# Seven block products for eight in the output product of two of four chunks, and low parts of input weights kept in memory

## What is computed

```python
h = _layer_norm(x) * (1 + scale[:, None]) + shift[:, None]
proj = h @ w_in
xa, ga, u, v, gb = jnp.split(proj, SPLITS, axis=-1)      # five times 512 columns
ya = _pool_mixer(xa, w_pool, pool_scale) * jax.nn.silu(ga)
yb = _sgu_mixer(jax.nn.gelu(u, approximate=False), jax.nn.gelu(v, approximate=False),
                sgu_ln_g, sgu_ln_b, w_sgu, b_sgu) * jax.nn.silu(gb)
y = jnp.concatenate([ya, yb], axis=-1) @ w_out
z = DEEPNORM_ALPHA * x + gate[:, None] * y
return _layer_norm(z) * ln_g + ln_b
```

## Time and profile before

| | us |
|---|---|
| median of 3 runs (673.91 to 674.61) | 673.99 |
| the profiled execution | 673.68 |
| its span in the profile | 671.6 |
| PE busy in the span | 659.8 (98%) |
| DVE busy | 516.1 (77%) |
| ACT busy | 235.1 (35%) |
| POOL busy | 61.7 (9%) |

### The profile page before, as it was taken

How to read it: one execution, slowest core, us unless ns; L and a number is a source line. 1 busy time by engine, 2 the same in 40 slices (tenths; PEclk the granted TensorE clock), 3 DMA queues, 4 the chain that set the end, 5 groups by cost and what they waited for, 6 DMA issues and landing times.

```text
span 671.6 us, 8845 instructions
## 1 busy us (share of the span) xinstructions
PE 659.8 (98%) x3103; PEld 551.3 (82%) x3103; DVE 516.1 (77%) x956; ACT 235.1 (35%) x307; POOL 61.7 (9%) x77
## 2 busy tenths in 40 slices
PE   8999999999999999999999999999999999999995
PEld 8888888877888888888888888888888888888884
DVE  5678898749969967766979968775977986656776
ACT  4424644316522333224722332322821333323300
POOL 2000110100002201100002201000002210000010
PEclk9999999999999999999999999999999999999999
DMA  8995643785334472288243562378343454224111
GB/s 340 365 332 233 219 153 116 163 228 189 125 111 141 126 258 86 95 116 322 96 156 100 180 248 65 106 94 332 102 148 90 162 205 159 104 79 154 52 63 62
DMA packets 34546, 108.73 MB, mean 162 GB/s; under 512 B 6573, under 2 KB 7633, under 8 KB 34514
## 3 DMA queue, kind: packets, MB, share of 16 engines
q1 hardware_dynamic: 34514, 108.31, 49.5%
HBM read 97.80 MB, written 10.50 MB: 161 GB/s over the span
## 4 chain that ended last, share of the span: by engine, by line
PE 95%; issue 2%; DVE 2%; ACT 0%; DMA 0%; POOLq 0%; POOL 0%; DVEq 0%
PE bank_b L1053 63%; PE bank_a L1053 25%; PE bank_a L1180 2%; PE bank_a L1140 1%; PE bank_b L1113 1%; PE bank_a L1171 1%; DVE w_low L656 1%; PE bank_b L1077 0%; DVE v_gelu L708 0%; PE bank_b L1171 0%; PE bank_b L1132 0%; PE bank_b L1104 0%; DMA vector_rows<-in_vectors 0%; ACT h_high L528 0%; ACT w_high L509 0%
## 5 line engine op out<-in xcount | busy, mean ns | idle before, releaser
L1053 PE MATMUL bank_b<-h_high,w_high 128*128 128x512 f32 x512 | 202.2, 395 | 0.2 <-DVE h_low L668 0.2
L1053 PE MATMUL bank_b<-h_low,w_high 128*128 128x512 f32 x512 | 199.3, 389 | 0.0
L1053 PE MATMUL bank_b<-h_high,w_low 128*128 128x512 f32 x512 | 199.3, 389 | 0.0
L661 DVE TENSOR_TENSOR w_low<-w_float,w_high 128x1024 fp32r<-128x1024 f32 x98 | 119.5, 1220 | 40.3 <-ACT w_high L518 40.2
L518 ACT ACTIVATE w_high<-w_float 128x1024 fp32r<-128x1024 f32 x98 | 103.4, 1056 | 130.5 <-DMA w_float<-in_w_units 57.2
L1053 PEld LDWEIGHTS bank_b<-h_high,w_high 128*128 128x128 f32 x512 | 96.2, 188 | 20.2 <-issue 1.1
L1053 PEld LDWEIGHTS bank_b<-h_high,w_low 128*128 128x128 f32 x512 | 96.1, 188 | 20.1
L1053 PEld LDWEIGHTS bank_b<-h_low,w_high 128*128 128x128 f32 x512 | 96.2, 188 | 19.5 <-issue 0.5
L461 POOL TENSOR_TENSOR z_rstd<-z_var_eps,minus_half 128x1 f32<-128x1 f32 x16 | 22.0, 1377 | 361.8 <-DVE z_var_eps L905 351.9
L1053 PE MATMUL bank_a<-w_high,y_high 128*128 128x512 f32 x128 | 49.9, 390 | 0.2 <-issue 0.2
L1053 PE MATMUL bank_a<-w_high,y_low 128*128 128x512 f32 x128 | 49.8, 389 | 0.0
(11 more groups left out here) (180 smaller groups left out, 934.0 us busy)
## 6 DMA issues: line engine op xcount, KB each, us to landing
w_float<-in_w_units SPq DMA_DIRECT2D x90, 512.0 KB, 3.4
x_norm<-in_x SPq DMA_DIRECT2D x16, 512.0 KB, 4.5
z<-in_x SPq DMA_DIRECT2D x16, 512.0 KB, 5.2
out<-z SPq DMA_DIRECT2D x15, 512.0 KB, 4.8
z<-in_mod_units SPq DMA_DIRECT2D x12, 512.0 KB, 9.1
x_norm<-in_x_channels SPq DMA_DIRECT2D x12, 512.0 KB, 15.0
w_float<-xa_units SPq DMA_DIRECT2D x12, 512.0 KB, 3.5
mod_spare<-in_mod_units SPq DMA_DIRECT2D x6, 512.0 KB, 8.6
```

Of the source, the lines that this page charges most:

```text
L661: vec.tensor_tensor(wL[:, n % S_SLOTS, :], w_float(c, n), wH[:, n % S_SLOTS, :].bitcast(F32), ALU.subtract).then_inc(w_low, 1)
L1053: last = mm(bank, wl if n == 2 else wh, ml if n == 1 else mh, start=start and n == 0, stop=stop and n == 2)
```

## The change

**Output product.** In chunks 1 and 2 (`FAST`) `y` and the weights are cut in 2 by 2 blocks: token halves of 256 by branches of 512 channels, and branches by output halves of 512 columns. Seven products of sums of blocks replace the eight of blocks. Each product is two units of 12 matmuls (`fast_unit`), so units 20 to 33 take the place of 20 to 27. A product writes two PSUM banks; products 4, 5 and 6 add to what product 2 or 3 has left there, after DVE has read it. DVE adds each product's banks to `z` (`add_parts`, two halves of a tile per product, four for the last). The gate is multiplied into the weights beforehand.

**Sums of weights.** POOL makes them once, after the gate rows are ready in chunk 0 (`prepare_out_units`: per quarter two multiplications of 128x1024 and four subtractions of 128x512). SP brings the raw weights (`prep_load`) and stores the seven results (`prep_store`, seven of 256 KB per quarter).

**Sums of y.** POOL makes four sums of 128x256 per head in chunks 1 and 2 (`sums_of_y`). The high and low parts of two of them are made at once, those of the other two later (`LATE_IN`).

**Low parts of input weights.** In chunk 0 SP stores the 20 low parts of units 0 to 19 (`store_low`). In chunks 1 to 3 ACT issues their load on its own queue just before it copies the high part; DVE makes no low part there, and PE waits for the landing.

**Order.** Loops are written out for the four chunks. In chunks 1 and 2 the work for the next `x` stands 2 to 4 iterations earlier, and the parts of `h` are spread over iterations 22 to 32.

```diff
+FAST = (1, 2)
+PRODUCTS = 7
+FAST_UNITS = IN_UNITS + 2 * PRODUCTS
+PARTS = ((0, 0, 0, 0), (0, 1, 1, 0), (1, 2, 2, 0), (1, 3, 3, 0), (2, 4, 0, 0), (2, 5, 1, 0), (3, 6, 2, 1), (3, 7, 3, 1),
+         (4, 4, 0, 1), (4, 5, 1, 1), (5, 6, 0, 1), (5, 7, 1, 1), (6, 4, 2, 1), (6, 4, 2, 0), (6, 5, 3, 1), (6, 5, 3, 0))
+READ_IN = {IN_UNITS + 3 + 2 * i: i for i in range(PRODUCTS - 1)}
...
+H_IN = {20: (0, 1), 21: (2, 3), 22: (4, 5), 23: (6, 7)}
+FAST_X_STATS_IN = {8: 0, 9: 1, 10: 2, 11: 3}
+FAST_X_ROWS_IN = 12
+FAST_X_CENTRE_IN = {16: (0, 1), 17: (2, 3), 18: (4, 5), 19: (6, 7)}
+FAST_H_IN = {22: (0,), 23: (1,), 24: (2,), 26: (3,), 28: (4,), 29: (5,), 30: (6,), 32: (7,)}
...
+                c, n = own(c, n)
+                held_c, held = (c, n - F_SLOTS) if n >= F_SLOTS or c == 0 else (c - 1, units(c - 1) + n - F_SLOTS)
+                if low_loaded(held_c, held):
+                    sp.wait_ge(w_high, base(held_c) + held + 1)
+                else:
+                    wait(sp, w_low, lows(held_c, held))
...
+                if c in FAST and n >= IN_UNITS:
+                    if c == FAST[0] and n == IN_UNITS:
+                        sp.wait_ge(out_stored, G * PRODUCTS * 16)
+                    source = out_units[(n - IN_UNITS) // 2, (n - IN_UNITS) % 2]
...
+
+            def store_low(n):
+
+                sp.wait_ge(w_low, max(n + 1, len(EARLY)))
+                stored = v_low_stored if n < V_UNITS else low_stored[n % S_SLOTS]
+                sp.dma_start(low_units[n], w_of(0, n)[1].bitcast(F32)).then_inc(stored, 16)
+
+            def prep_load(q):
+
+                if q == 0:
+                    sp.wait_ge(w_low, XA_ALONE[-1] + 1)
+                elif q == 1:
+                    sp.wait_ge(sgu_done, G)
+                else:
+                    sp.wait_ge(out_stored, (q - 1) * PRODUCTS * 16)
+                for half in range(2):
+                    sp.dma_start(prep_tile(q, half), w_units[IN_UNITS + half * G + q]).then_inc(prep_landed[q % 2][half], 16)
+
+            def prep_store(q):
+
+                sp.wait_ge(prep_ready, q + 1)
+                zero, one = prep_tile(q, 0), prep_tile(q, 1)
+                for i, half_unit in enumerate((zero[:, 0:T], t4[:, :], zero[:, T:], t12[:, 0:T], t12[:, T:], one[:, 0:T],
+                                               one[:, T:])):
+                    cut = slice(q % 2 * T, (q % 2 + 1) * T)
+                    sp.dma_start(out_units[i, q // 2][:, cut], half_unit).then_inc(out_stored, 16)
...
+                    if first and FIRST_LOOP <= n + AHEAD < IN_UNITS:
+                        store_low(n + AHEAD)
                     if first and n in (12, 13):
                         store_xa(n - 10)
                     if first and n == UNITS - 1:
                         sp.wait_ge(xa_stored, G * 16)
...
+                    if first and n in (23, 25, 27):
+                        prep_store((23, 25, 27).index(n))
+                    if c == 1 and n == 1:
+                        prep_store(G - 1)
                     if last and 6 <= n < 6 + 4:
 
...
+            def prepare_out_units():
+
+                gp = nc.gpsimd
+                pool.wait_ge(gate_ready, 2)
+                for q in range(G):
+                    prep_steps.begin(q)
+                    zero, one = prep_tile(q, 0), prep_tile(q, 1)
+                    for half, t in enumerate((zero, one)):
+                        rows = t.rearrange("p (b n) -> p b n", b=2)
+                        gate = gateB[:, half * HALF:(half + 1) * HALF].rearrange("p (o n) -> p o n", o=1)
+                        pool.wait_ge(prep_landed[q % 2][half], (q // 2 + 1) * 16)
+                        done = gp.tensor_tensor(rows, rows, gate.broadcast_to([P, 2, T]), ALU.mult)
+                    prep_steps.then(pool, done)
+                    b21, b11, b22, b12 = zero[:, 0:T], zero[:, T:], one[:, 0:T], one[:, T:]
+                    wait(pool, out_stored, q * PRODUCTS * 16)
+                    prep_steps.then(pool, gp.tensor_tensor(t12[:, 0:T], b12, b11, ALU.subtract))
+                    prep_steps.then(pool, gp.tensor_tensor(t12[:, T:], b22, t12[:, 0:T], ALU.subtract))
+                    gp.tensor_tensor(t4[:, :], b21, t12[:, T:], ALU.subtract)
+                    gp.tensor_tensor(b12, b22, b12, ALU.subtract).then_inc(prep_ready, 1)
+
+            def sums_of_y(c, g):
+
+                gp, nth, half = nc.gpsimd, FAST.index(c) * G + g, T // 2
+                if nth == 0:
+                    pool.wait_ge(out_stored, G * PRODUCTS * 16)
+                pool.wait_ge(ys_ready, c * G + g + 1)
+                pool.wait_ge(yp_ready, c * G + g + 1)
+                pool.wait_ge(ys_low, c * G + g)
+                a12, a22 = y_float(c, g)[:, 0:half], y_float(c, g)[:, half:]
+                a11, a21 = mixed[:, 0:half], mixed[:, half:]
+                gp.tensor_tensor(s12[:, 0:half], a21, a22, ALU.add).then_inc(s_steps, 1)
+                pool.wait_ge(s_steps, nth + 1)
+                gp.tensor_tensor(s12[:, half:], s12[:, 0:half], a11, ALU.subtract).then_inc(s12_ready, 1)
+                gp.tensor_tensor(s34[:, g, 0:half], a11, a21, ALU.subtract)
+                pool.wait_ge(s12_ready, nth + 1)
+                gp.tensor_tensor(s34[:, g, half:], a12, s12[:, half:], ALU.subtract).then_inc(s34_ready, 1)
+
             def chunk(c, first, last):
                 if not first:
...
+                if c in FAST:
+                    x_rstds(c + 1, 0)
+                    x_rstds(c + 1, 1)
+                    sums_of_y(c, 0)
+                    x_rstds(c + 1, 2)
+                    x_rstds(c + 1, 3)
+                    for g in range(1, G):
+                        sums_of_y(c, g)
...
+                if first:
+                    prepare_out_units()
...
             def split_high(c, n):
 
-                wait(act, unit_done, c * UNITS + n - S_SLOTS + 1)
...
-                nc.scalar.activation(wH[:, n % S_SLOTS, :], w_float(c, n), ACT.Copy).then_inc(w_high, 1)
+                if low_loaded(c, n):
+                    if c == 1 and n < S_SLOTS:
+                        act.wait_ge(low_stored[n], (IN_UNITS // S_SLOTS - 1) * 16)
+                        act.wait_ge(v_low_stored, V_UNITS * 16)
+                    nc.scalar.dma_start(w_of(c, n)[1].bitcast(F32), low_units[n])\
+                        .then_inc(low_landed[(base(c) + n) % S_SLOTS], 16)
+                nc.scalar.activation(w_of(c, n)[0], w_float(c, n), ACT.Copy).then_inc(w_high, 1)
...
+                        if n == ys_in[g] and c not in FAST:
                             act.wait_ge(ys_ready, c * G + g + 1)
                             nc.scalar.activation(yH[:, G + g, :], mixed[:, :], ACT.Copy).then_inc(ys_high, 1)
+                        if n == ys_in[g] and c in FAST:
+                            act.wait_ge(ys_ready, c * G + g + 1)
+                            nc.scalar.activation(aH[:, g, :], mixed[:, 0:T // 2], ACT.Copy)
+                            act.wait_ge(s12_ready, FAST.index(c) * G + g + 1)
+                            nc.scalar.activation(yH[:, G + g, :], s12, ACT.Copy).then_inc(ys_high, 1)
+                    if c in FAST and n in LATE_IN:
+                        g = LATE_IN[n]
+                        act.wait_ge(unit_done, base(c) + IN_UNITS + 4)
+                        act.wait_ge(s34_ready, FAST.index(c) * G + g + 1)
+                        nc.scalar.activation(yH[:, g, :], s34[:, g, :], ACT.Copy).then_inc(s34_high, 1)
...
+                c, n = own(c, n)
+                if low_loaded(c, n):
+                    return
+                dve.wait_ge(w_high, base(c) + n + 1)
+                if c == 0:
+                    dve.wait_ge(low_stored[n % S_SLOTS], min(n // S_SLOTS - 1, IN_UNITS // S_SLOTS - 1) * 16)
+                high, low = w_of(c, n)
+                vec.tensor_tensor(low, w_float(c, n), high.bitcast(F32), ALU.subtract).then_inc(w_low, 1)
...
+            def late_low(c, g):
+                dve.wait_ge(s34_high, FAST.index(c) * G + g + 1)
+                vec.tensor_tensor(yL[:, g, :], s34[:, g, :], yH[:, g, :].bitcast(F32), ALU.subtract).then_inc(s34_low, 1)
+
+            def add_parts(c, i):
+
+                nth = FAST.index(c) * len(PARTS)
+                dve.wait_ge(unit_done, base(c) + IN_UNITS + 2 * i + 2)
+                for p, (product, bank, j, half) in enumerate(PARTS):
+                    if product != i:
+                        continue
+                    cut = slice(half * HALF, (half + 1) * HALF)
+                    psum = (A, B)[bank // 4][:, bank % 4, :]
+                    earlier = [o for o in range(p) if PARTS[o][2:] == (j, half)]
+                    if earlier:
+                        dve.wait_ge(part_read, nth + earlier[0] + 1)
+                        ins = vec.tensor_tensor(z[:, j, cut], psum, z[:, j, cut], ALU.add)
+                    else:
+                        dve.wait_ge(z_landed[j], (c + 1) * 16)
```

(40 more changed lines are left out.)

223 lines of the change are left out of this document (156 added, 67 removed).

## The result

The changed kernel takes 718.72 us (median of 4 runs, 716.32 to 719.26), the kernel before 673.95 on the same chip: ratio 1.0658, interval 1.0631 to 1.0685. The forecast was 671.6, the range ended at 680.5. The profiled execution has a span of 717.5 us against 671.6.

What follows compares the result with a forecast made beforehand. PE was taken as the bound, busy 98% of the span. 671.6 - 10.9 + 5.8 + 1.0 + 0.5 + 1.2 = 669.2 us of span, so a median of 671.6; range 662.5 to 680.5.

Steps and rivals of the forecast that it cites:

- Matmuls, -10.9: Output products of chunks 1 and 2: 168 matmuls each for 192, 48 fewer at 0.2266 us, all on the path.
- Load loop, +5.8: Weight loads in the short products: PE ends each some 2.7 us late, taken as 2.9, twice.
- The round of 5.6 us: Two float slots for weights: load 3.4, copy 1.05, subtraction 1.15 us as the least time for two units.
- the line through the two select rows: POOL's work priced from 0.29 us for 128 columns and 0.96 for 512, so 1.74 ns a column.
- Rival 2: Short units: DVE too full, each chunk loses 5.8 us, total 677.4; sign, DVE without idle time; chance 0.10.
- Low parts loaded, +1.0: Low parts loaded over ACT's queue: weights behind `x_channels` come later, 0.5 us per chunk in chunks 1 and 2.
- so 3.4 + 0.4 of the 6.6 goes: Load behind `x_channels`, unit 17: its 6.6 us lead shrinks because the low part is asked for after the float part lands.
- Start of chunk 0, +0.5: DVE waits until four low parts of `v` are stored, against 1.65 us of slack at unit 10; bounds 0 and 3.
- Sums on POOL, +1.2: POOL's sums of weights in chunk 0, 30 us in all, hidden except where POOL and DVE hold each other up.
- rows 13 show POOL as the one that gives way: Trace rows: a POOL power takes 1.50 us beside a DVE subtraction, 0.56 alone; used to put POOL's cost near 0.
- Rival 1: DVE waits for POOL instruction by instruction: PE stands 7.5 us at unit 23, 8.5 in all, total 678.9; chance 0.27.
- DVE waits for that, some 5 us: DVE waits for POOL's `z_rstd` of chunk 0 behind quarter 3 of the sums, hidden by 10 us of slack.

Runs made afterwards that it cites:

- run 14: Run 12's kernel, in the short products 896 of 1024 columns of ACT's copies and DVE's subtractions left out, loads whole: 684.52 us, ratio 1.0164.
- run 12: Changed kernel with rows ordered by ACT, POOL's sums moved later, low parts of units 8 to 19 only, unit 23 and third product's banks early: 696.76 us.
- run 3: Changed kernel without the stores of x's mean and rstd rows for chunks 2 and 3, stale rows read instead: 702.92 us, ratio 1.0423.
- run 5: Kernel before the change plus POOL's four multiplications and eight subtractions on dead tiles from about 152 us, no transfers: 686.63 us, ratio 1.0193.
- run 1: Changed kernel without POOL's multiplications and subtractions on the output weights, all loads and stores kept: 698.08 us, ratio 1.0364.
- run 16: Seven products in chunk 2 only, four float slots, POOL's sums paced by PE's units, rows by ACT, low parts of units 8 to 19: 671.43 us, ratio 0.9969.
- run 6: Changed kernel with one row store of 256 runs of 16 bytes, DVE reading the row tiles with a step of four: 716.19 us, ratio 1.0622.
- run 8: Of the change only the stored and loaded low parts, with the old output products and no sums on POOL: 679.66 us, ratio 1.0094.

## Why the prediction was wrong, point by point

- **Matmuls, -10.9: right.** 48 are gone, and 168 take 38.28 us when nothing holds them (run 14), 5.24 less than the 192.
- **Load loop, +5.8: mis-sized.** The short products took 46.76 and 46.45 us where 38.07 is bare PE, so the term, slow matmuls with it, was 8.7 + 8.4 = 17.1, not 5.8. The step that failed here is "Counting from the start of unit 20: tanh, gate and product of the last head end at 2.2". In the changed kernel unit 20 starts at 340.24; tanh ran on time at 340.44, but DVE, behind with its work on x, came to the gate at 345.07, and unit 23's low part ended near 351.6, 11.4 us after unit 20's start and not 6.6. The round of 5.6 us was about right as a least value: in chunk 2 of run 12 the low parts of every second unit start 5.6 to 6.5 us apart. The waits for bank reads (1.9 and 1.7 us at their longest) were not in the sum. POOL's additions of 256 columns took 0.74 us, not 0.5: the line through the two select rows priced all of POOL's work too low (a subtraction of 512 columns 1.29 alone, not 0.96). Rival 2's sign did not come: DVE was busy for 35.8 of the 46.8 us.
- **Low parts loaded, +1.0: wrong.** The step that failed is "so 3.4 + 0.4 of the 6.6 goes": a low part asked for behind the row stores was priced at the usual landing of 3.4 us. It took 17.8 in chunk 1 and 17.5 in chunk 2, and with the clock this cost 15.8 us in all (run 3). The earlier trace rows held the sign: the load issued at 290.57, 4.8 us behind the last of the same row stores (285.82), landed 16.2 us later, and I took that for the place and not for the price of a landing there. The unit hit was 15, not 17. What I had weighed, bandwidth, was not the trouble. "ACT gains 60 issues of about 0.35 us at 35% busy: nothing" held for 59 of them; the one of 7.81 us is not seen to have cost PE anything.
- **Start of chunk 0, +0.5: mis-sized**, 5.4 (2.2 to 5.4 over the runs that store the low parts of v). DVE waited 4.21 us for the stores of v's low parts, against an upper bound of 3.
- **Sums on POOL, +1.2: wrong, 20.6, the largest miss.** The step that failed is "rows 13 show POOL as the one that gives way". They show one short power beside one DVE instruction, not a row of long additions. Rival 1 had the mechanism and the Trainium skill's rule, page "SBUF — State Buffer", section "SBUF: two separate sides". Its 7.5 us of standing for the first bout are close to the gap of 6.75; that its 8.5 in all are near the stage's loss of 8.90 is luck, since it had no clock in it (2.0 us here), and POOL's work alone cost 13.1 in run 5. The trace agrees with that rule on DVE's side too, 2.10 and 2.82 us against 0.68, and with its condition: the instruction with an input in PSUM was not held. Still rival 1's total of 678.9 was 40 too low: the other terms were, and POOL's lateness cost chunk 1 as well, as the next point says.
- **"Quarter 0 ... its stores stand in iteration 23: no wait" and "DVE waits for that, some 5 us": wrong.** POOL waited 20.8 us for out_units stores at 199.64, DVE 21.2 for `z_rstd` at 236.31, and SP's blocked queue held weight loads. Without POOL's arithmetic (run 1) the channel units of chunk 1 gave back 8.8 us and its v units 0.4; this is part of the 20.6.
- **The clock was in no term.** I priced waits by their length; 18.4 of 56.8 us lost were matmuls at the lower level behind them.
- **"I am wrong if PE waits in the input units of chunks 1 to 3 for anything but unit 17": so it was.**

Open stays why the start varied between 2.2 and 5.4 us with the same stores, and which of the sums' stores and loads cost the v units of chunk 1 the 3.3 us that run 1 left.

## What to carry to other kernels

A kernel with PE at 98% has no slack that a share of busy time would show: before work is moved to an "idle" engine, look for what it shares with the busy ones (here POOL's and DVE's reads of SBUF, and transfers queued behind small stores) in the very stretch where it will run. Spread such work, as run 16 did with one or two instructions per unit of the bounding engine, and don't put it in a block. When units get shorter, check the round that feeds them against the new length, and price gaps by more than their length, since the clock can fall behind them: here half as much again on average. Price a landing by the rows of the place where it will be asked for, not by the median of the page, and before a long issue is called the cause, look whether the gap is there without one. When an experiment's median hardly moves, compare its stages: in run 6 a gain of 15 us was hidden by new losses.

## What the runs showed of the hardware

- Two row stores of 512 single numbers each held up the transfers behind them, on SP's and ACT's queue alike: a low part landed 17.5 to 18.7 us after its issue, and 15.4 in run 8, against 9.3 to 10.2 (chunk 1) once the rows went as 256 runs of 16 bytes, and 4.0 to 9.0 without the stores. Meanwhile DMA moved 19 GB/s at a busy share of 0.75.
- The issues behind such stores were long in chunk 1 (11.3 us for four on SP, 7.81 for one on ACT) and not in chunk 2 (1.93 and 0.33); the landings were late in both.
- DVE with two SBUF inputs of 512 columns: 0.68 us alone, 1.6 to 2.9 beside POOL; with a PSUM input 0.68 either way. POOL's multiplication of 1024 columns took 2.4 us alone and near 3.0 beside DVE (160.54, two in 6.06).
- A DVE input read with a step of four elements: 1.07 us against 0.69 for 512 columns. ACT's copy of 512 columns with such a step took 1.09 to 1.14.
- After 9.96 us without work PE ran at 1.2 GHz for about five microseconds, and so it did after 4.57 us; after 2.74 us its clock did not fall.
